# Operands of the compression matmuls kept by token phase, and the operand area begun at a multiple of 512 bytes

## The reference

```python
def compress_tokens(t, pos, w1, w2):
    b, s, g, d = t.shape
    nc = (s - COMP_BLOCK) // COMP_STRIDE + 1        # 31 windows
    idx = np.arange(nc)[:, None] * COMP_STRIDE + np.arange(COMP_BLOCK)[None, :]
    blocks = t[:, idx] + pos.astype(t.dtype)[None, None, :, None, :]
    flat = blocks.transpose(0, 1, 3, 2, 4).reshape(b, nc, g, COMP_BLOCK * d)
    return jax.nn.gelu(flat @ w1) @ w2

kc = compress_tokens(k_cmp, cmp_pos[0], cmp_w1[0], cmp_w2[0])
vc = compress_tokens(v_cmp, cmp_pos[1], cmp_w1[1], cmp_w2[1])
```

## Time and profile before

| | |
|---|---|
| median of three executions | 2194.51 us |
| the profiled execution | 2193.54 us |
| its span, first to last instruction | 2191.8 us |
| mean granted clock of TensorE | 0.995 |
| TensorE busy | 2135.2 us, 97% |
| VectorE, ScalarE, GpSimd busy | 1295.3, 872.1 and 132.3 us |
| chain that ended last | TensorE 85%, VectorE 9%, ScalarE 2% |
| moved by DMA | 203.72 MB |

### The profile page before, as it was taken

One profiled execution on the slowest core, in us unless ns is written; L12 is line 12 of the kernel. 1 busy time (PEld: TensorE's weight loads), 2 busy tenths in 40 slices (PEclk: granted clock), 3 DMA queues, 4 the chain that ended last, 5 costly groups with the idle time before them and its releaser, 6 DMA issues.

```text
span 2191.8 us, 29263 instructions
## 1 busy us (share of the span) xinstructions
PE 2135.2 (97%) x11544; PEld 1740.7 (79%) x11544; DVE 1295.3 (59%) x2291; ACT 872.1 (40%) x1534; POOL 132.3 (6%) x149
## 2 busy tenths in 40 slices
PE   8999989999999999998999999999999999999998
PEld 6877769888888978885678888888898888888887
DVE  4267766877765687636763787765575555333323
ACT  4156664543431354426652543442141234222221
POOL 0000002000000200002410200000020011000001
PEclk9999999999999999999999999999999999999999
DMA  8110002333346323320003233226423322222332
GB/s 277 58 39 21 25 16 76 98 96 97 93 156 219 103 92 106 95 88 20 1 20 96 68 116 96 94 85 241 168 68 97 96 78 87 96 96 92 91 87 68
DMA packets 61096, 203.72 MB, mean 93 GB/s; under 512 B 6944, under 2 KB 9504, under 8 KB 60704
## 3 DMA queue, kind: packets, MB, share of 16 engines
q1 hardware_dynamic: 58944, 194.51, 27.7%
q10 hardware_dynamic: 2016, 7.34, 1.1%
HBM read 197.63 MB, written 2.10 MB: 91 GB/s over the span
## 4 chain that ended last, share of the span: by engine, by line
PE 85%; DVE 9%; ACT 2%; POOL 1%; issue 1%; DMA 0%; SPq 0%; DVEq 0%; ACTq 0%
PE bank L736 24%; PE bank L740 24%; PE bank L738 24%; POOL h L640 1%; PE bank L1129 1%; DVE pbuf L2018 1%; PE bank L917 1%; DVE wlo L1723 1%; PE bank L1012 1%; PE bank L1135 1%; PE bank L989 1%; DVE xlo L1737 1%; PE bank L1152 1%; DVE pbuf L2037 1%; PE bank L681 1%
## 5 line engine op out<-in xcount | busy, mean ns | idle before, releaser
L736 PE MATMUL bank<-xhi,whi 128*128 128x512 f32 (+1 forms) x1848 | 706.8, 382 | 18.4 <-DVE xlo L1737 9.6
L738 PE MATMUL bank<-xlo,whi 128*128 128x512 f32 (+1 forms) x1848 | 698.9, 378 | 0.0
L740 PE MATMUL bank<-xhi,wlo 128*128 128x512 f32 (+1 forms) x1848 | 698.8, 378 | 0.0
L1273 ACT ACTIVATE whi<-raw 128x1024 fp32r<-128x1024 f32 (+1 forms) x321 | 333.4, 1040 | 742.1 <-PE bank L740 717.2
L1723 DVE TENSOR_TENSOR wlo<-raw,whi 128x1024 fp32r<-128x1024 f32 (+1 forms) x321 | 389.7, 1215 | 299.1 <-ACT whi L1273 298.7
L736 PEld LDWEIGHTS bank<-xhi,whi 128*128 128x128 f32 x1848 | 347.0, 188 | 95.6 <-issue 14.2
L740 PEld LDWEIGHTS bank<-xhi,wlo 128*128 128x128 f32 x1848 | 346.8, 188 | 72.0
L738 PEld LDWEIGHTS bank<-xlo,whi 128*128 128x128 f32 x1848 | 347.2, 188 | 70.1
L736 PE MATMUL bank<-hid_hi,whi 128*128 128x512 f32 (+1 forms) x624 | 226.2, 362 | 0.0
L740 PE MATMUL bank<-hid_hi,wlo 128*128 128x512 f32 (+1 forms) x624 | 224.5, 360 | 0.0
L738 PE MATMUL bank<-hid_lo,whi 128*128 128x512 f32 (+1 forms) x624 | 224.1, 359 | 0.0
(11 more groups left out here) (274 smaller groups left out, 2497.1 us busy)
## 6 DMA issues: line engine op xcount, KB each, us to landing
raw<-w SPq DMA_DIRECT2D x297, 512.0 KB, 3.5
ada_w<-w_ada SPq DMA_DIRECT2D x64, 384.0 KB, 3.9
raw<-w SPq DMA_DIRECT2D x24, 384.0 KB, 3.3
w_k<-w_cmp ACTq DMA_DIRECT2D x1, 2048.0 KB, 10.4
w_v<-w_cmp ACTq DMA_DIRECT2D x1, 2048.0 KB, 7.9
out_t<-h SPq DMA_DIRECT2D x16, 128.0 KB, 1.7
h<-xT ACTq DMA_DIRECT2D x4, 256.0 KB, 5.2
h<-xT SPq DMA_DIRECT2D x4, 256.0 KB, 6.9
```

What stands on the lines that cost most here:

```text
L736: pe.matmul(bk[:, tok], whi[w][:, cols], hi[:, k, tok], start=k == 0, stop=False, skip_group_check=split)
L738: pe.matmul(bk[:, tok], whi[w][:, cols], lo[:, k, tok], start=False, stop=False, skip_group_check=split)
L740: return pe.matmul(bk[:, tok], wlo[w][:, cols], hi[:, k, tok], start=False, stop=last, skip_group_check=split)
L1273: act.activation(whi[g % SLOTS][:, 0:n], raw[g % RAWS][:, 0:n], ACT.Copy).then_inc(s_hi, 1)
```

## The change

`dk`, `dv` and `stg` get another layout. A token t*16 + m*2 + q (t from 0 to 31, m from 0 to 7, q 0 or 1) has the phase (q, m). `stg` now holds for each panel two rows of 272 floats, one for each q, and in a row 8 runs of 34 floats, one for each m: 32 tokens of this phase and 2 position columns. `nsa_take` writes this order, so it reads `bank` and `rstd_b` with a step of 16 floats in its innermost dimension. The transfers copy the row q = 0 to the lower half of the partitions and q = 1 to the upper, 272 floats each in place of 512 or 511. The moving operand of `compress_in` becomes 4 groups x 33 neighbouring floats. The number of matmuls and their shapes stay as they are.

The position vectors leave the parameter block `par` and come by a transfer of their own, `pos_t` (64 floats per partition), issued by SyncE behind `hpar`. Four small copies put them in `stg`, in place of two into `dk` and `dv`; ScalarE, in place of TensorE, waits for them. The semaphore for the inputs is waited for with 48 in place of 32.

`arena` is rounded up to a multiple of 512 bytes: to byte 95744. Three buffers of the SSD part (`usum`, `after`, `vbuf1`) move by 256 bytes within it.

```diff
@@
-        arena = base[0]
+        arena = (base[0] + 511) // 512 * 512
@@
-        DW = 544
-        dk = sb("dk", [P, 4, DW], F32, at(48))
-        dv = sb("dv", [P, 4, DW], F32, at(56.5))
+        WIN = 32
+        PW = 8 * (WIN + 2)
+        dk = sb("dk", [P, 4, PW], F32, at(48))
+        dv = sb("dv", [P, 4, PW], F32, at(52.25))
+        stg = sb("stg", [P, 4, 2, PW], F32, at(56.5))
+        pos_t = sb("pos_t", [P, NPOS], F32, at(120))
@@
             sp.dma_start(par[:, 64:NPAR], params[:, 64:NPAR]).then_inc(s_in, 16)
             sp.dma_start(hpar[:, 0:2], heads).then_inc(s_in, 16)
+            sp.dma_start(pos_t[:, :], params[:, NPAR:NPAR + NPOS]).then_inc(s_in, 16)
@@
-                pe.wait_ge(s_pos, 2)
                 pe.wait_ge(s_ev, kv + 1)
                 w1, dup = (w1_k, dk) if kv == 0 else (w1_v, dv)
                 for hh in range(2):
                     for m in range(16):
+                        at_ = (m % 8) * (WIN + 2) + m // 8
                         mm = pe.matmul(bank[kv][:, hh * 132:(hh + 1) * 132], w1[:, m, hh * P:(hh + 1) * P],
-                                       dup[:, :, 2 * m:2 * m + 16 * 32 + 1:16], start=m == 0, stop=m == 15)
+                                       dup[:, :, at_:at_ + WIN + 1], start=m == 0, stop=m == 15)
@@
+                act.wait_ge(s_pos, 2 * kv + 2)
                 act.wait_ge(s_ev, taken(2 * kv + 1))
                 for half in range(2):
                     for a in range(2):
-                        act.dma_start(dup[half * HD:(half + 1) * HD, a:a + 3:2, 0:S - half],
-                                      stg[a * HD:(a + 1) * HD, 2 * kv:2 * kv + 2, half:S]).then_inc(s_dup[kv], 16)
+                        act.dma_start(dup[half * HD:(half + 1) * HD, a:a + 3:2, :],
+                                      stg[a * HD:(a + 1) * HD, 2 * kv:2 * kv + 2, half, :]).then_inc(s_dup[kv], 16)
@@
+                if c < V_FIRST:
+                    to = stg[:, c, :, :].rearrange("p q (m t) -> p q m t", m=8)[:, :, :, 0:WIN]
+                    dve.tensor_tensor(to, by_phase(bank[b][:, :]), by_phase(rstd_b[:, :]), ALU.mult)\
+                        .then_inc(s_ev, 1)
+                    return
```

More of the change, by code:

```diff
@@ L171 @@
 PARAMS = [("gains", 64), ("gains2", 32), ("ssd_w", CH * 4), ("ssd_b", CH), ("ffn_w", 2 * 44 * 3), ("ffn_b", 2 * 44),
-          ("dskip", NZ), ("norm_w", NZ), ("c", KD), ("ada_b", 48), ("pos", 32), ("w2", 256), ("cw", 8 * 3)]
+          ("dskip", NZ), ("norm_w", NZ), ("c", KD), ("ada_b", 48), ("w2", 256), ("cw", 8 * 3)]
 COL = {}
@@ L178 @@
 NPAR = _n
+NPOS = 64
 def step_of(s):
@@ L320, in build @@
         w1_v = sb("w1_v", [P, 16, 256], F32, at(99))
-        stg = sb("stg", [P, 4, S], F32, at(115))
         pbuf = sb("pbuf", [P, 3, 4, S], F32, at(83))
@@ L348, in build @@
         ebuf = sb("ebuf", [P, 2, S], F32, at(26))
-        usum = sb("usum", [P, P], F32, at(129.5))
-        after = sb("after", [P, P], F32, at(130))
-        vbuf = [sb("vbuf0", [P, S], F32, where["ssum"]), sb("vbuf1", [P, S], F32, at(127.5)),
+        usum = sb("usum", [P, P], F32, at(129.25))
+        after = sb("after", [P, P], F32, at(129.75))
+        vbuf = [sb("vbuf0", [P, S], F32, where["ssum"]), sb("vbuf1", [P, S], F32, at(127.25)),
                 sb("vbuf2", [P, S], F32, at(124.25)), sb("vbuf3", [P, S], F32, at(120))]
@@ L1410, in _ @@
                 square(h[:, j, :], j, s_pa, 0)
-            act.wait_ge(s_in, 32)
+            act.wait_ge(s_in, 48)
             chain(act.activation(csil[:, :], par[:, COL["c"]:COL["c"] + KD], ACT.Silu))
@@ L1945, in _, with by_phase @@
             square_sums(0, 0)
-            dve.wait_ge(s_in, 32)
+            dve.wait_ge(s_in, 48)
             dve.wait_ge(s_const, 1)
-            for kv, dup in enumerate((dk, dv)):
-                pos = par[:, COL["pos"] + 16 * kv:COL["pos"] + 16 * kv + 16]
-                dve.tensor_copy(dup[:, :, S:DW:2], pos.unsqueeze(1).to_broadcast([P, 4, 16])).then_inc(s_pos, 1)
+            for c in range(V_FIRST):
+                pos = pos_t[:, 32 * (c // 2):32 * (c // 2) + 32]
+                to = stg[:, c, :, :].rearrange("p q (m t) -> p q m t", m=8)[:, :, :, WIN:WIN + 2]
+                dve.tensor_copy(to, pos.rearrange("p (q m j) -> p q m j", q=2, m=8)).then_inc(s_pos, 1)
+            def by_phase(x):
+                return x.rearrange("p (t m q) -> p q m t", m=8, q=2)
             def nsa_take(c, b):
                 dve.wait_ge(s_pe, c + 1)
+                if c < V_FIRST:
[3 more added lines that the diff above has]
+                    return
                 if c == GATES:
                     dst, rows = gt[:, :], 48
-                elif c < V_FIRST:
-                    dst, rows = stg[:, c, :], P
                 elif c in K_PANEL:
@@ L2508, in pack @@
         + [cols(np.repeat(v["ssd_d"][0], HD)), cols(v["ssd_norm_w"][0]), cols(v["c_2"][0]), cols(v["ada_b_2"][0]),
-           v["nsa_cmp_pos"][0].reshape(2, 16, 2, HD).transpose(2, 3, 0, 1).reshape(P, 32),
            v["nsa_cmp_w2"][0].reshape(2, 2, P, HD).transpose(2, 0, 1, 3).reshape(P, 256),
-           taps(v["conv_w_2"][0], KD)], 1)
+           taps(v["conv_w_2"][0], KD),
+           np.concatenate([v["nsa_cmp_pos"][0].reshape(2, 2, 8, 2, HD).transpose(4, 0, 3, 2, 1).reshape(HD, 64)] * 2)], 1)
     return {
```

## The result

The changed kernel takes 2176.57 us (median of five, 2173.2 to 2178.73), beside 2192.92 us before (five, 2191.18 to 2196.32). The ratio is 0.9923, with a 95% interval from 0.9908 to 0.9937: 0.77% faster, 16.9 us by the ratio (the two medians are 16.4 us apart). The profiled execution took 2176.18 us, with a span of 2174.4 us where it was 2191.8 us.

The account below looks back on a forecast made before the run. TensorE, busy 97% of the span, was taken as the bound, in `compress_in` by its own matmul pace. 2193.54 - 14.0 = 2179.5 us, with the median 0.97 us above: 2180.5 us forecast, range 2173 to 2188.

Parts of the forecast that it names:

- The matmuls: Compression matmuls in both `compress_in` calls: 113.4 ns a start in place of 223, 14.0 us less over 128 instructions.
- near 290: Sign in the profile after: durations of the compression matmuls near 290 ns, with 64 instructions in about 7.3 us per group.
- only part: Rival, 8%: odd starts and run ends make half of the compression matmuls keep their pace; 7 us are left, 2187.5 us.
- the pace stays: Rival, 6%: something else, such as a 206 ns weight load, holds the compression matmuls at 223 ns; 2194.5 us.
- The takes: VectorE's four takes, now reading with a 64-byte step: 0 to 0.7 us more each, hidden by cover, cost 0.
- the four copies: Position copies on VectorE, four for two: 2.9 us of cover for two copies more, each below 0.91 us.
- the `pos_t` transfer: One issue more on SyncE ahead of panel 3, 0.43 us, against 1.3 us of cover before TensorE.
- Cost: 0: Moving `arena` from 416 to 0 bytes behind a multiple of 512 costs nothing; exchanged operand roles showed the same pace.
- a rival at 3%: Rival, 3%: the new address quickens the fp32r stream by 18 ns per 512 columns, 4728 matmuls, 85 us; about 2095 us.
- a pace moved by more than 1 ns: Sign that the forecast is wrong: the fp32r matmuls' 233 ns from start to start moves by more than 1 ns.
- The stretch at half clock around 1000 us: Blur on the forecast: some 10 us at 1.2 GHz; 4.4 us could come back at full clock, as much be lost elsewhere.

## Why the prediction was right, and where it was not

- **The matmuls.** Forecast: 113.4 ns a start and 14.0 us. Measured: 111.3 ns and 14.3 us; alone, at the old address, the layout gave a ratio of 0.9936, the forecast ratio to the hundredth of a per cent. Four columns more than L1118 cost about 1 ns. Of the signs, the duration of 274 ns is below the "near 290" expected. That the step caused the 223 ns is shown by the runs with other steps.
- **The rivals "only part" and "the pace stays".** Both fell with the first row of the profile after. The weight load of 206 ns was, as argued, a result of the slower matmul: it takes 188 now.
- **What is hidden.** The takes got 0.38 us dearer each (bounds 0 to 0.7), the four copies 0.96 us together, and the `pos_t` transfer cost one issue. None reached TensorE, and tripled takes did not either.
- **The address, "Cost: 0".** This is the step that was wrong. The argument was that the V stretch, with the roles of the operands exchanged, has the same pace. But exchanging the roles keeps the pair of places, 416 and 128; if it is the pair that counts, the V stretch of one kernel can't show it. The comparison tested the wrong thing, and so a rival at 3% was closest to the truth in kind, with a wrong reason against it. The prediction priced this rival at 85 us, for an area at 0; a multiple of 512 gave 3.5 us by itself, and the next 128 bytes gave 33 more. It also counted 4728 matmuls where the stream has 6600: those with `hid`, `y`, `o` and `yc` as operands and the V stretch belong to it. Its own sign, a pace moved by more than 1 ns, was just not met: 233.3 became 232.3. The 215.7 ns that this rival takes from the Trainium skill stand on the page TensorE: Matmul & The Clock Gate in its section "Wait — 56ns, not 53.3ns?", not in the section named; no fp32r stream here came below 226.6 ns.
- **Luck.** The address was put at nothing with a wrong argument, and that this did no harm is luck of the address chosen. The same layout gave 2185.66 us at 288, 2176.57 at 0 and 2143.6 at 128; the last is 29 us below the range of the prediction.
- **The remaining microseconds.** The change gave 16.9 us by the ratio: 14.3 from the compression and about 3 from the address (ratios 0.9936 at the old one, 0.9923 and 0.9915 at the new, 0.9984 for the address alone). The clock gives little of it. The stretch at half clock around 1000 us was shorter, 3.4 us in place of 10.2, but the one around 1100 us was longer, 10.2 us in place of twice 3.4, and another of 3.4 us appeared in the attention: before the last 10 us of the program these are 17 us in either profile. A single stretch can move more: around 1000 us TensorE's lead over the kernel before grew by 2.6 us, and it lost about 1 us at each of the other two. The second profile did not have the one in the attention. The windows 291.5 to 295 us of the first and of the second profile of the changed kernel:

```profile
291.50:295.00 3.50, 3.50 (x22) 2.94 (x24) 1.73 (x8) 2.63 (x8) 0.00 (x0) 0.51 0.01 2
```

```profile
291.50:295.00 3.50, 2.40 (x26) 1.93 (x28) 2.65 (x16) 3.20 (x10) 0.00 (x0) 1.00 0.01 2
```

The granted clock is at 1.2 GHz in the one and at 2.4 GHz in the other, in the attention, where TensorE waits now and then for VectorE and ScalarE. So this stretch came in one execution and not in another of the same kernel, while those near 980 and 1100 us came in both.

## What to carry to other kernels

In these runs a float32 moving operand whose columns lay 16 bytes or more apart made TensorE half as fast; if a faster layout can be written by an engine that has time, write it there, and pay the scattered access where it is hidden. Before believing that a shift of buffers costs nothing, compare runs at a few addresses: here 128 bytes were worth more than the whole rewrite, and a layout that shrinks a neighbouring buffer can lose half of its gain by moving everything behind it. A control that swaps two operands says little on what their places do together.

## What the runs showed that was not expected

The fp32r stream has no single pace: around 500 us it ran at 234.2, 233.3, 232.3 or 226.8 ns per 512 columns at a granted clock of 2.4 GHz, according to where in the row the stationary and the moving operands lie. 226.6 to 226.8 ns came with a distance of 0 or 256 bytes modulo 512, with durations of 389 ns for all of 230 matmuls, where the change spreads over 390 to 404 ns. The pace of 232.3 ns of the change held in some stretches and gave way to 233.3 in another. Matmuls of 256 columns have another order: 113.7 ns with the area at 64, 118.6 at 0 and 119.6 at 128. Why the places matter is not settled by these runs, nor whether the place of the area alone would do. The best kernel of this study is the one with the fixed buffers at 384 and the area at 128, 2141.53 us, 2.4% below the kernel before; the other two kernels at this pace are within its interval.
